# Linear attention's log decay sums as fp32r products of two parts; the gate's bias as a seventeenth row

## The reference, cut to what matters

```python
log_a = log_sigmoid(ga @ w_alpha_up + b_alpha) / 16      # ga: [256,16], w_alpha_up: [16,512]
# per head, S_t = diag(exp(log_a_t)) S_{t-1} + k_t^T v_t,  o_t = q_t S_t   (causal)
# so score[i,j] = sum_d q[i,d] k[j,d] exp(sum of log_a[u,d] for u in (j, i])   for j <= i
```

## Time and profile before

| | |
|---|---|
| median of 3 runs | 2674.42 us (2671.24 to 2674.51) |
| the profiled execution | 2671.07 us, of which the span in the profile is 2669.0 us |
| PE, weight loads | 2615.9 us (98%), 2298.5 us (86%) |
| DVE, ACT, POOL | 1601.6 us (60%), 1306.7 us (49%), 84.7 us (3%) |
| granted TensorE clock, mean | 0.996 |
| read from memory | 504.39 MB, 190 GB/s over the span |

### The profile page before, as it was taken

One profiled execution on the slowest core, in us unless ns is written; L12 is line 12 of the kernel. 1 busy time (PEld: TensorE's weight loads), 2 busy tenths in 40 slices (PEclk: granted clock), 3 DMA queues, 4 the chain that ended last, 5 costly groups with the idle time before them and its releaser, 6 DMA issues.

```text
span 2669.0 us, 37336 instructions
## 1 busy us (share of the span) xinstructions
PE 2615.9 (98%) x13344; PEld 2298.5 (86%) x13344; DVE 1601.6 (60%) x1640; ACT 1306.7 (49%) x1545; POOL 84.7 (3%) x61
## 2 busy tenths in 40 slices
PE   8999999999999999999999999998999999999998
PEld 7988788888888888888888889887789999998887
DVE  5557655556655544544555655587677767776555
ACT  5445555454445444444444554554655545444444
POOL 0000000000000000000000000021000000000000
PEclk9999999999999999999999999999999999999999
DMA  7665555576666666666666666543456666666664
GB/s 244 198 196 166 175 172 173 174 214 224 199 196 191 203 196 197 198 199 200 196 203 201 198 190 196 158 134 123 154 174 203 199 201 200 197 203 202 202 202 158
DMA packets 233286, 507.67 MB, mean 190 GB/s; under 512 B 15829, under 2 KB 18229, under 8 KB 232436
## 3 DMA queue, kind: packets, MB, share of 16 engines
q1 hardware_dynamic: 231712, 499.31, 62.2%
q0 software_dynamic: 1360, 7.21, 0.8%
q10 hardware_dynamic: 132, 0.03, 0.0%
HBM read 504.39 MB, written 2.10 MB: 190 GB/s over the span
## 4 chain that ended last, share of the span: by engine, by line
PE 92%; DVE 4%; ACT 3%; issue 1%; DMA 0%; DVEq 0%; ACTq 0%; SPq 0%
PE ps L372 20%; PE ps L374 20%; PE ps L373 20%; PE ps L361 18%; PE ps L362 9%; DVE wlo L1318 1%; ACT whi L854 1%; PE ps L439 1%; PE ps L735 0%; PE ps L743 0%; DVE area_d L1466 0%; PE ps L676 0%; DVE temp L1751 0%; ACT hT L901 0%; PE ps L507 0%
## 5 line engine op out<-in xcount | busy, mean ns | idle before, releaser
L1318 DVE TENSOR_TENSOR wlo<-raw,whi 128x1024 fp32r<-128x1024 f32 x944 | 1172.5, 1245 | 995.0 <-ACT whi L854 987.3
L854 ACT ACTIVATE whi<-raw 128x1024 fp32r<-128x1024 f32 x944 | 997.3, 1057 | 1287.1 <-PE ps L374 905.5
L361 PE MATMUL ps<-hT,whi 128*128 128x512 f32 x2304 | 757.9, 383 | 6.5 <-DVE wlo L1318 4.3
L372 PE MATMUL ps<-whi,hT 128*128 128x512 f32 x1792 | 694.8, 388 | 8.2 <-ACT big L959 2.4
L373 PE MATMUL ps<-wlo,hT 128*128 128x512 f32 x1792 | 681.4, 380 | 0.0
L374 PE MATMUL ps<-whi,hT 128*128 128x512 f32 x1792 | 681.3, 380 | 0.0
L362 PE MATMUL ps<-hT,wlo 128*128 128x256 f32 x2304 | 628.0, 273 | 0.0
L361 PEld LDWEIGHTS ps<-hT,whi 128*128 128x128 f32 x2304 | 435.4, 189 | 68.8 <-issue 4.9
L362 PEld LDWEIGHTS ps<-hT,wlo 128*128 128x128 f32 x2304 | 442.3, 192 | 0.1
L372 PEld LDWEIGHTS ps<-whi,hT 128*128 128x128 f32 x1792 | 340.3, 190 | 60.2 <-issue 4.1
L373 PEld LDWEIGHTS ps<-wlo,hT 128*128 128x128 f32 x1792 | 340.2, 190 | 49.1 <-issue 2.6
(11 more groups left out here) (246 smaller groups left out, 1077.9 us busy)
## 6 DMA issues: line engine op xcount, KB each, us to landing
raw<-w_ffn_in SPq DMA_DIRECT2D x352, 512.0 KB, 3.7
raw<-w_in SPq DMA_DIRECT2D x304, 512.0 KB, 4.2
raw<-w_ffn_out SPq DMA_DIRECT2D x176, 512.0 KB, 4.6
raw<-w_o_ret SPq DMA_DIRECT2D x32, 512.0 KB, 4.6
raw<-w_out SPq DMA_DIRECT2D x32, 512.0 KB, 4.6
raw<-w_o SPq DMA_DIRECT2D x32, 512.0 KB, 3.6
raw<-w_o_attn SPq DMA_DIRECT2D x16, 512.0 KB, 4.5
resid<-x SPq DMA_DIRECT2D x8, 256.0 KB, 6.0
```

The costliest lines, as they stand in the source:

```text
L361: pe.matmul(acc, whi[:, c % SLOTS, f], in_turn(hT[:, kt, :, :]), start=(kt == 0), stop=False)
L372: pe.matmul(acc, hi, w_hi, start=start, stop=False)
L854: act.activation(whi[:, c % SLOTS, :], raw[:, c % SLOTS, :], ACT.Copy).then_inc(hi_ready, 1)
L1318: dve.tensor_tensor(wlo[:, c % SLOTS, :], raw[:, c % SLOTS, :], whi[:, c % SLOTS, :].bitcast(F32), ALU.subtract).then_inc(lo_ready, 1)
```

## The change

The change does four things.

1. The zero level is gone. There are seven levels and one of 128 columns for the half: 1024 columns of sums instead of 1152. Its place in the score products is taken by the raw keys and queries of the half. `qe`, `ke` and the multiplications of DVE and POOL have seven levels instead of eight.
2. The sums are fp32r products of two parts: ACT copies `log_a` to `la_hi` (fp32r) at step 4 of the second `gv` block, DVE writes `la_lo = log_a - la_hi` at step 5, for all heads at once; ACT copies the zero and one matrices to fp32r (`sums_r`) between the sections `gqk` and `dqk` with three copies of 1536 columns in all. A half takes four products of 128x512. POOL's copies to `la_h` and its wait on `g_sum` go. ACT takes one exponential of 1024 columns instead of 1024 and 128.
3. The bias lies in row 16 of the right side of the low-rank product, and `gaT` has a seventeenth row of ones (DVE fills rows 0 to 31 with 1.0 before it writes the sixteen): two float32 products instead of four.
4. The `ga` product reads its moving operand through `in_turn`; ACT and DVE read its sums through `halves_of`.

```diff
@@ TensorE
-            gaT = temp[0:16, 0:SEQ]
+            gaT = temp[0:17, 0:SEQ]
...
-                pe.matmul(ps[:, 0, :], ga_hi[:, f], hT[:, kt, :, :], start=(kt == 0), stop=False)
+                pe.matmul(ps[:, 0, :], ga_hi[:, f], in_turn(hT[:, kt, :, :]), start=(kt == 0), stop=False)
...
-                        pe.matmul(ps[:, 6 + t, :], gaT[:, t * P:t * P + P], area_g[0:16, 0:512], start=True, stop=False)
-                        mm = pe.matmul(ps[:, 6 + t, :], ones[0:1, :], area_g[0:1, 512:1024], start=False, stop=True)
+                        mm = pe.matmul(ps[:, 6 + t, :], gaT[:, t * P:t * P + P], area_g[0:17, 0:512], start=True, stop=True)
...
-                        pe.wait_ge(S("g_la"), h + 1)
+                        pe.wait_ge(S("g_la"), 1)
...
-                    la = la_h[:, t * P:t * P + P]
-                    for n in range(2):
-                        pe.matmul(ps[:, 4 + n, :], la, sums_m[:, n * 512:n * 512 + 512], start=True, stop=True)
-                    pe.matmul(ps[:, 6, 0:P], la, sums_m[:, LW + t * P:LW + t * P + P], start=True, stop=True)\
-                        .then_inc(S("g_sum"), 1)
+                    for la in (la_hi, la_lo):
+                        for n in range(2):
+                            mm = pe.matmul(ps[:, 4 + n, :], la[:, t * 512 + h * P:t * 512 + h * P + P], in_turn(sums_r[n + n * t]),
+                                           start=(la is la_hi), stop=(la is la_lo))
+                    mm.then_inc(S("g_sum"), 1)
...
+                        own = slice(n * P, n * P + P)
+                        left = ke[:, own] if n < LEVELS - 1 else tiles_b[:, 4 + h, t * P:t * P + P]
+                        right = qe[:, own] if n < LEVELS - 1 else tiles_b[:, h, t * P:t * P + P]
+                        mm = pe.matmul(ps[:, 4 + n // 4, n % 4 * P:n % 4 * P + P], left, right, start=True, stop=True)
@@ ScalarE
+            act.wait_ge(S("second_in"), 16)
+            act.activation(flat_e[:, 2048:3072], sums_m[:, 0:1024], ACT.Copy)
+            act.activation(flat_e[:, 3072:3072 + 3 * P], sums_m[:, 4 * P:7 * P], ACT.Copy)
+            act.activation(flat_e[:, 3072 + 3 * P:3584], sums_m[:, 1024:], ACT.Copy).then_inc(S("sums_r"), 1)
...
+                if k == 4:
+                    act.wait_ge(S("g_log"), 1)
+                    act.activation(la_hi, temp[:, 1024:2048], ACT.Copy).then_inc(S("la_hi"), 1)
...
-                    act.activation(decays[:, 0:LW].rearrange("p (n c) -> p n c", n=2), ps[:, 4:6, :], ACT.Exp, scale=1.0 / 16)
-                    act.activation(decays[:, LW:], ps[:, 6, 0:P], ACT.Exp, scale=1.0 / 16).then_inc(S("g_exp"), 1)
+                    act.activation(halves(decays.rearrange("p (n c) -> p n c", n=2)), halves_of(ps[:, 4:6, :]), ACT.Exp, scale=1.0 / 16)\
+                        .then_inc(S("g_exp"), 1)
@@ VectorE
+            own(dve.memset(temp[0:32, 0:SEQ], 1.0))
...
+                if k == 5:
+                    dve.wait_ge(S("la_hi"), 1)
+                    dve.wait_ge(S("sums_r"), 1)
+                    dve.tensor_tensor(la_lo, log_a, la_hi.bitcast(F32), ALU.subtract).then_inc(S("g_la"), 1)
...
-                    dve.tensor_tensor(qe.rearrange("p (n c) -> p n c", c=P), lev, q.to_broadcast([P, LEVELS, P]), ALU.mult)
+                    dve.tensor_tensor(qe[:, 0:LW - P].rearrange("p (n c) -> p n c", c=P), lev, q.to_broadcast([P, LEVELS - 1, P]), ALU.mult)
@@ GpSimd
-            pool.dma_start(area_g[0:1, 512:1024], a["b_alpha_2"]).then_inc(S("alpha_in"), 16)
+            pool.dma_start(area_g[16:17, 0:512], a["b_alpha_2"]).then_inc(S("alpha_in"), 16)
...
-            pool.wait_ge(S("g_log"), 1)
...
-                pool.tensor_copy(temp[:, 768:1024].rearrange("p (t n) -> p t n", t=NT), la[:, :, bass.ds(h * P, P)])\
-                    .then_inc(S("g_la"), 1)
...
-                    pool.tensor_tensor(ke, lev, tiles_b[:, bass.ds(4 + h, 1), t * P:t * P + P].to_broadcast([P, LEVELS, P]), ALU.mult)\
+                    pool.tensor_tensor(ke, lev, tiles_b[:, bass.ds(4 + h, 1), t * P:t * P + P].to_broadcast([P, LEVELS - 1, P]), ALU.mult)\
```

More of the change, by code:

```diff
@@ L78, in shape_constants @@
         masks.append((u // (2 * s) == t // (2 * s)) & ((u // s) % 2 == 0) & right)
-    sums.append(np.zeros((P, P)))
     masks.append(np.eye(P))
@@ L138, in two_blocks @@
         first = sb("first", [P, 2 * P + NT * SEQ])
-        masks = sb("masks", [P, 10 * P + LW])
+        masks = sb("masks", [P, 9 * P + LW])
         gains = sb("gains", [P, GAIN_ROWS])
@@ L175, in two_blocks @@
         ga_hi, ga_lo = flat_e[:, 0:3 * P], flat_e[:, 512:512 + 3 * P]
+        la_lo, la_hi = flat_e[:, 0:1024], flat_e[:, 1024:2048]
+        sums_r = [flat_e[:, 2048:2560], flat_e[:, 2560:3072], flat_e[:, 3072:3584]]
         ps = ctx.enter_context(nc.psum_tensor("ps", [P, 8, 512], F32))
@@ L703, in _ @@
                 f = slice(kt * 16, kt * 16 + P)
-                pe.matmul(ps[:, 0, :], ga_hi[:, f], hT[:, kt, :, :], start=(kt == 0), stop=False)
-                mm = pe.matmul(ps[:, 0, 0:SEQ], ga_lo[:, f], hT[:, kt, 0, :], start=False, stop=(kt == KT - 1))
+                pe.matmul(ps[:, 0, :], ga_hi[:, f], in_turn(hT[:, kt, :, :]), start=(kt == 0), stop=False)
+                mm = pe.matmul(ps[:, 0, 0:SEQ], ga_lo[:, f], in_turn(hT[:, kt, 0, :]), start=False, stop=(kt == KT - 1))
             mm.then_inc(S("ga_mm"), 1)
@@ L723, in _ @@
             ke, qe = area_g[:, 0:LW], area_g[:, LW:2 * LW]
-            sT, cross, la_h = temp[:, 0:512], temp[:, 512:768], temp[:, 768:1024]
+            sT, cross = temp[:, 0:512], temp[:, 512:768]
             def linear_attention(c, h):
@@ L1144, in _ @@
             act.wait_ge(acc_freed, base["gv"] + 1)
-            act.activation(lo_sum[0:16, 0:SEQ], ps[0:16, 0, SEQ:], ACT.Copy).then_inc(lo_copied, 1)
+            act.activation(halves(lo_sum[0:16, 0:SEQ]), halves_of(ps[0:16, 0, SEQ:]), ACT.Copy).then_inc(lo_copied, 1)
             z_abs = free_c[:, 0:1024]
@@ L1161, in _ @@
                 late_rows(gv, ACT.Copy)(base["gv"] + n, 1 - n, n)
-            decays = free_c[:, 0:9 * P]
+            decays = free_c[:, 0:LW]
             junk_g = rows_d[:, :, 1024:1024 + SEQ]
@@ L1714, in _ @@
             dve.wait_ge(lo_copied, n_cols + 1)
-            own(dve.tensor_tensor(temp[0:16, 0:SEQ], ps[0:16, 0, 0:SEQ], lo_sum[0:16, 0:SEQ], ALU.add))
+            own(dve.memset(temp[0:32, 0:SEQ], 1.0))
+            own(dve.tensor_tensor(halves(temp[0:16, 0:SEQ]), halves_of(ps[0:16, 0, 0:SEQ]), halves(lo_sum[0:16, 0:SEQ]), ALU.add))
             own(dve.tensor_tensor(temp[0:16, 0:SEQ], temp[0:16, 0:SEQ], scale_row[0:16, :], ALU.mult))
@@ L1758, in linear_attention @@
                         dve.wait_ge(S("g_o"), h)
-                    own(dve.tensor_tensor(decays[:, 0:LW].rearrange("p (n c) -> p n c", n=2), ps[:, 4:6, :],
+                    own(dve.tensor_tensor(decays.rearrange("p (n c) -> p n c", n=2), ps[:, 4:6, :],
                                           masks_m.rearrange("p (n c) -> p n c", n=2), ALU.mult))
@@ L2025, in _ @@
                 pool.dma_start(free_c[:, 1280 + n * SEQ:1280 + (n + 1) * SEQ], a[name].to_broadcast([P, SEQ])).then_inc(S("norms_in"), 16)
-            la = temp[:, 1024:2048].rearrange("p (t n) -> p t n", t=NT)
-            lev = free_c[:, 0:LW].rearrange("p (n c) -> p n c", c=P)
-            ke = area_g[:, 0:LW].rearrange("p (n c) -> p n c", c=P)
-            pool.wait_ge(S("g_log"), 1)
+            lev = free_c[:, 0:LW - P].rearrange("p (n c) -> p n c", c=P)
+            ke = area_g[:, 0:LW - P].rearrange("p (n c) -> p n c", c=P)
             def linear_attention(h):
-                pool.tensor_copy(temp[:, 768:1024].rearrange("p (t n) -> p t n", t=NT), la[:, :, bass.ds(h * P, P)])\
-                    .then_inc(S("g_la"), 1)
                 for t in range(NT):
                     pool.wait_ge(S("g_exp"), 2 * h + t + 1)
-                    pool.tensor_tensor(ke, lev, tiles_b[:, bass.ds(4 + h, 1), t * P:t * P + P].to_broadcast([P, LEVELS, P]), ALU.mult)\
+                    pool.tensor_tensor(ke, lev, tiles_b[:, bass.ds(4 + h, 1), t * P:t * P + P].to_broadcast([P, LEVELS - 1, P]), ALU.mult)\
                         .then_inc(S("g_k"), 1)
-            linear_attention(0)
-            with pool.Fori(1, G_HEADS) as h:
-                pool.wait_ge(S("g_sum"), 2 * h)
+            with pool.Fori(0, G_HEADS) as h:
                 linear_attention(h)
```

10 lines of the change are left out of this document (4 added, 6 removed).

## The result

The kernel after takes 2659.31 us at the median of 6 runs (2657.86 to 2664.69); before it was 2673.99 in 6 runs taken beside them (2671.24 to 2676.07). The ratio is 0.9952, with an interval from 0.9942 to 0.9962: faster by 14.7 us. The forecast was 2658, range 2653 to 2667. The profiled execution took 2660.32 us, against 2671.07 before.

A forecast was written before the change was run, and what follows sets the result against it. PE was taken to bound the kernel, busy 98% of the span. Gains of 8.7 + 5.25 + 0.2 = 14.2 us gave 2656.9 or 2660.2 by the two starting times; it predicted 2658 us, range 2653 to 2667.

The forecast's parts named there:

- Sums on PE: Sums of each half: four fp32r products cost 0.86 us instead of 1.94, 1.08 less per half, 8.6 for eight halves.
- the new products might run at the float32 rate: Rival at the sums: 0.86 us per product, 6 us slower overall, 2677 to 2680; turns at about 0.68; chance 0.02.
- First halves: t = 0 halves: ACT's table load limits heads 0 and 1 to 0.58 us each; head 2 0.78, head 3 1.08, plus 0.4s.
- The 0.42: Chain from sums to scores: DVE and POOL take 7/8 of the elements, POOL 3.40 becomes 2.98 us, gaining 0.42.
- The waits: Linear attention gains 8.7 us; PE waits 0.9 before scores of heads 0 and 1, 0.3 in head 2, 3.8 last.
- the 0.4s: Two PE waits of 0.4 us in front of `linear_out` vanish, 0.8 together, counted at heads 2 and 3, t = 0.
- The low-rank product: Its cost falls from 7.15 to 1.90 us, the clock fall behind it gone: gain 5.25, other end 1.7.
- `ga`: The `ga` product: sixteen records at 0.394 us median against 0.38 elsewhere; gain between 0.2 and nothing, taken as 0.2.
- Added copies: Copies for `la_hi`, `la_lo` and matrices cost zero, at worst 1.6 us; `la_lo` ready 2.8 us before PE asks.
- the fall behind the last wait: Rival: the clock fall behind the 4.4 us wait goes too, 1.7 us, giving 2655 to 2658; chance 0.13.
- the one at the low-rank product: Rival: the clock still falls at the low-rank product; sum 10.6 us, 2660.5 to 2664; chance 0.22.
- the waits kept 0.6, not most: Rival: waits keep most of the sums' gain, the sums giving 5 instead of 8.7 us, 2660.5 to 2664; chance 0.10.

The follow-up runs named there:

- eight_levels: The kernel after, but DVE and POOL again multiply all eight levels, the eighth result unused: 2661.34 us, ratio 0.9958.
- f32_sums: The kernel after, but sums as float32 products of the unsplit `log_a`, still 1024 columns, without the copies of matrices and parts: 2666.67 us, ratio 0.9977.
- bias_row: The kernel before, with only the bias folded in as a seventeenth row of the low-rank product: 2669.0 us, ratio 0.9987; second profile 2672.7 us.
- the pads: Two kernels after, each low-rank product made twice or preceded by an overwritten 128-row float32 product: 2661.51 and 2661.66 us.
- sums_only: The kernel after, but with the old low-rank product and the bias as a product of its own: 2663.77 us, ratio 0.9964.
- pad_few: The kernel after, with each 17-row low-rank product made twice: 2661.51 us, ratio 0.9963; profiled again at 2665.84 us.

## Why the prediction was right, and where it was off

**Sums on PE: right.** 0.86 us, 1.08 less per half, as worked out from 0.216 per product. That the new products might run at the float32 rate is refuted by their records. (The price per product at which that rival turns is 21.5 / 32 = 0.67 us, not 0.68: 8 x 1.94 + 6 is 21.5.)

**First halves: right, with a wrong picture of POOL.** 0.58 in head 0 and 0.59 in head 1, by ACT's table load. On DVE both terms came as reckoned in head 0: `qe` starts 1.06 us behind the exponential's start instead of 1.22 (0.16), and from there to the end of `cross` it is 3.19 instead of 3.61 (0.42). POOL's own record says something else: it starts 1.31 behind the exponential instead of 1.28 and lasts 2.79 instead of 3.40. The 0.42 is not POOL's alone. In eight_levels 0.13 of it lay in `qe` (1.22 against 1.09) and 0.28 in POOL's own work (2.39 against 2.11). An eighth of POOL's 3.40 was the right size all the same, since that record begins 0.06 behind `qe` and so spans nearly all the work of both.

**The waits: mis-sized.** Linear attention was to give 8.7 and gave 8.1. Half by half it gave 0.58, 1.08, 0.59, 1.07, 1.23, 0.99, 1.26 and 1.28, where 0.58, 1.08, 0.58, 1.08, 1.18, 1.08, 1.48 and 1.65 were forecast (the 0.4s counted to the half behind them). So 0.37 is missing in the last half and 0.22 in head 3's t = 0. The latter is the wait in front of `linear_out`, which was to give 0.4 and gave 0.2. The same wait in front of head 2 gave only 0.2 as well, but there it cost nothing, since the scores behind it were to wait 0.3 for the chain: PE came 0.2 later than forecast and waited only 0.06. Head 1's scores were to wait 0.9 and waited 0.5, counted from where PE was free (1748.49 + 0.22 to 1749.23). The prediction had carried head 0's rows over to head 1. In the kernel before, PE stood 0.38 in front of head 0's scores and only 0.03 in front of head 1's (1754.42 to 1754.45). That changes the wait and not the gain.

The two shortfalls have one cause, the chain in the t = 1 halves. The exponential of the last half starts 1.22 behind the sums, not 1.07, since ACT is in a split when they end. From there to the end of the wait it is 6.59 instead of 6.95: 0.36 of the 0.58. The rest is the order of DVE and POOL. Second half of head 0, timelines of the kernel before:

```profile
1735.04 1.23 DVE L1750 TENSOR_TENSOR area_g<-big 128x1024 f32<-128x1024 f32 x1 [0.79 <-ACT big L1170]
1735.09 3.41 POOL L2036 TENSOR_TENSOR area_g<-big 128x1024 f32<-128x1024 f32 x1 [10.69 <-ACT big L1170]
1736.18 2.47 DVE L1751 TENSOR_TENSOR temp<-big 128x128 f32<-128x128 f32 x1
```

and after:

```profile
1729.35 1.01 ACT L1178 ACTIVATE big<-ps 128x1024 f32<-128x1024 f32 x1
1729.48 1.23 DVE L1327 TENSOR_TENSOR wlo<-raw,whi 128x1024 fp32r<-128x1024 f32 x1 [1.36 <-ACT whi L856]
...
1730.55 2.11 POOL L2046 TENSOR_TENSOR area_g<-big 128x896 f32<-128x896 f32 x1 [9.69 <-ACT big L1178]
1730.62 2.98 DVE L1764 TENSOR_TENSOR area_g<-big 128x896 f32<-128x896 f32 x1
...
1733.53 0.28 DVE L1765 TENSOR_TENSOR temp<-big 128x128 f32<-128x128 f32 x1
```

Before, DVE was free when the exponential ended, so its `qe` went first and POOL waited for it. Now the exponential ends while DVE still subtracts for `wlo`. POOL goes first and takes 2.11, DVE's `qe` takes 2.98 instead of 1.09 and ends 0.94 behind POOL, and `cross` comes last, alone. From the start of the exponential to the end of `cross` it is 4.46 us; in the t = 0 half, where DVE goes first, 4.25 (1716.76 to 1721.01). In f32_sums, where the sums end later and DVE goes first again (POOL 2.90), the same t = 1 half takes 4.25 as well (1730.07 to 1734.32), so it is the order and not the half. These 0.21 and the 0.15 of the later exponential are the 0.36 that the last half lacks. In front of `linear_out` the chain so moves by 1.29 where PE moves by 1.08, and takes 0.2 off a wait of 0.4, as measured. In f32_sums, with the order of before, the last wait is the 3.8 that was forecast.

The prediction had this pattern in its hands: `cross` with an eighth of the elements took twice the time of `qe` and ended 0.15 behind POOL. It read from it that POOL sets the end, and not that the two engines exclude each other, so that their order can cost. The Trainium skill (SBUF — State Buffer, "SBUF: two separate sides") states that a DVE operation with two inputs in SBUF and a GpSimd operation that reads SBUF share a port pair under an exclusive lock, held by whoever starts first for the whole instruction. The durations agree with it. In the second half it is 2.98 - 1.09 = 1.89 us longer for `qe` behind a POOL operation that ran 2.04 us beyond its start.

**The low-rank product: right.** 5.05 against 5.25: 3.4 for the clock, 1.65 for two products less, and the same 5.05 in both profiles of bias_row. The missing 0.2 is the changeover to 17 rows and back, which was taken as 0.18 and is 5.34 - 14 x 0.216 - 0.216 - 1.72 = 0.38. The argument for it was weaker than its outcome. It leaned on 188.6:194, a stretch with low activity and no fall; in the kernel after, the same work did fall (192:197, 0.66). One execution without a fall does not show that a stretch has none: of the 14 profiles, 9 have a fall there and 5 have none. What bears the argument out are the pads and the eight profiles without a fall behind 1.98 us.

By the rule of the Trainium skill that was weighed (TensorE: Matmul & The Clock Gate, "Part 1: The HAM clock gate"), which warns of idle gaps alone, the gain was to be 1.7. The trace does not agree: the falls before, in sums_only and in pad_few come behind gapless records. The same section of the Trainium skill says that the clock's activity window runs free, so that one kernel shows a different number of slow products from run to run. The differing falls of one kernel's executions agree with that (for bias_row, 6.8 us behind the mark in one profile and 10.3 in the other).

**`ga`: undersized.** 0.36 instead of 0.2. The records fell from 394 to 382 ns at the median, but what counts is their spacing, first to last start 4.9 us instead of 5.3. In bias_row, which has the old `ga` product, the stretch from there to the product in front of the low-rank one is 28.69 us, against 28.70 before and 28.34 after, so the 0.36 is this edit's.

**Added copies: hidden, as reckoned.** Timeline of ACT after, the matrices behind `gqk`:

```profile
1581.35 1.06 ACT L1145 ACTIVATE split_e<-masks 128x1024 fp32r<-128x1024 f32 x1
1582.31 0.51 ACT L1146 ACTIVATE split_e<-masks 128x384 fp32r<-128x384 f32 x1
1582.71 0.30 ACT L1147 ACTIVATE split_e<-masks 128x128 fp32r<-128x128 f32 x1
1582.91 1.05 ACT L856 ACTIVATE whi<-raw 128x1024 fp32r<-128x1024 f32 x1
1584.35 1.06 ACT L856 ACTIVATE whi<-raw 128x1024 fp32r<-128x1024 f32 x1 [0.39 <-PE ps L363]
```

Two splits later ACT idles again, and PE did not wait. `la_lo` is done at 1711.03, 3.1 us before the sums (2.8 forecast).

**The sum.** 14.2 was forecast and 13.5 measured in the stretch of the change; the medians differ by 14.7 and 14.6 in two sets of runs. In net it is 9.8 and 10.1, with the low-rank fall's 3.4 again 13.2 and 13.5. The 1.1 between 13.5 and the medians is within what falls elsewhere do to a median, and the agreement of 14.2 with the medians is partly luck. Of the rivals, the fall behind the last wait stayed, the one at the low-rank product did not come back, and the waits kept 0.6, not most. The forecast of 2658 lies between two sums, 2656.9 and 2660.2, by the two starting times; that it came within 1.3 of the median is luck in the same measure.

## What to carry to other kernels

Count the falls of the clock in short stretches before two executions are compared: here they set two profiles of one kernel 4.8 us apart in a question of 14, while times cleared of them agreed within 0.4 in three pairs of four. Better still, measure an edit between two rows that enclose it: the same stretch agreed within 0.04 us in all kernels that share its code, where no fall lay in it. In these traces 3.5 us of float32 products of few rows without a break cost 1.7 or 3.4 us more than their length, and behind 2 us of them the clock did not fall; so fold a bias into a spare row. Where DVE and GpSimd multiply at the same moment, look at which of them starts first. When a large wait is removed, look at those behind it: without the wait of 4.2 us a later one grew from 2.4 to 3.3, and the gain was 2.2 to 2.5 us in net, which the median of five runs did not show. With the wait in between shortened too, the median was 4.3 us better.

## What the runs showed of the hardware that was not expected

- GpSimd's 128x896 multiplication lasts 2.11 us when it starts first and 2.79 when DVE's 128x896 starts 0.25 before it; DVE's lasts 1.09 first and 2.98 second.
- The clock fell behind gapless 16- and 17-row products in 4 of 4 profiles, for 1.7 or 3.4 us, and never behind 4 us of float32 products half of which had 128 rows (2 profiles).
- The same instructions of the first block, near 192:197, ran at 1.00 in 5 profiles and with a fall of 1.7 us in 9.
- A fall near the start cost less than its 1.7 us: the early mark came at 33.93 to 34.16 in the 6 profiles with one near 11:16, and at 33.37 to 33.82 in the 8 without. In after against before (34.16, 33.40), PE's waits for `wlo` in front of the mark were 0.7 shorter in all.
- A fall that begins in a wait costs less than its clock says: in bias_row 3.4 us were lost at 1826:1834, with PE waiting until 1828.41, and net, which takes off all 3.4, makes the edit 0.85 us better than its own stretch shows (2.5 against 1.65).
